# Two layers of mixed attention on one NeuronCore: another order of the paired attention steps

## The reference

```python
for layer in range(2):
    h = rmsnorm(x, norm_attn[layer]); proj = h @ w_in[layer]
    # four mixers of 4 heads each, head width 64
    o_sb = stick_breaking(q, k, v)   # a = exp(log_sigmoid(z) + suffix sums of -softplus(z)), strictly causal
    o_mb = softmax(q k^T * scale + bias, causal) @ v             # "moba": with 256 tokens its own block only
    o_ns = g0 * o_cmp + g1 * o_slc + g2 * o_win                  # one k/v head for each branch, sigmoid gates
    # cmp: keys and values from gelu(blocks @ w1) @ w2, 15 compressed positions
    o_df = rmsnorm((softmax1 - lam * softmax2) @ v) * (1 - lambda_init)
    x = x + concat(o_sb, o_mb, o_ns, o_df) @ w_out[layer]
    h2 = rmsnorm(x, norm_mlp[layer])
    x = x + relu(h2 @ w_up[layer])**2 @ w_down[layer]
x = rmsnorm(x, final_norm)
# second model: an mLSTM layer and a latent attention layer on x and 256 context tokens;
# each is steered by a modulation (silu(c) @ ada_w + ada_b), which does not depend on x
```

## Time and profile before

| | |
|---|---|
| median of three runs | 2309.01 us |
| time of the profiled execution | 2308.36 us |
| its span on the core | 2306.4 us |
| TensorE busy | 2208.7 us, 96% |
| VectorE busy | 1342.5 us, 58% |
| ScalarE busy | 1184.9 us, 51% |
| granted TensorE clock, mean | 0.99 of full |
| moved by DMA | 312.28 MB, 135 GB/s |

### The profile page before, as it was taken

How to read it: one execution, slowest core, us unless ns; L and a number is a source line. 1 busy time by engine, 2 the same in 40 slices (tenths; PEclk the granted TensorE clock), 3 DMA queues, 4 the chain that set the end, 5 groups by cost and what they waited for, 6 DMA issues and landing times.

```text
span 2306.4 us, 33632 instructions
## 1 busy us (share of the span) xinstructions
PE 2208.7 (96%) x13550; PEld 1833.3 (79%) x13550; DVE 1342.5 (58%) x2206; ACT 1184.9 (51%) x2004; POOL 0.2 (0%) x4
## 2 busy tenths in 40 slices
PE   8899999979999999999999999999999998899998
PEld 8669999849999777887677676868888876668998
DVE  5766645685654655445666654366666345546764
ACT  4665534575544654444344443266655336446764
POOL 0000000000000000000000000000000000000000
PEclk9899999989999999999999999999999999999999
DMA  8545575753576213222112121212223222214542
GB/s 307 203 182 182 215 307 197 280 204 131 182 291 241 91 55 114 87 100 98 58 73 73 73 74 46 101 70 95 92 93 108 92 73 92 92 38 150 184 169 101
DMA packets 45719, 312.28 MB, mean 135 GB/s; under 512 B 4951, under 2 KB 7255, under 8 KB 8580
## 3 DMA queue, kind: packets, MB, share of 16 engines
q1 hardware_dynamic: 45572, 310.20, 36.8%
HBM read 309.11 MB, written 1.07 MB: 134 GB/s over the span
## 4 chain that ended last, share of the span: by engine, by line
PE 82%; DVE 11%; ACT 5%; issue 2%; DMA 0%; ACTq 0%; DVEq 0%; SPq 0%
PE bank L792 62%; PE bank L797 8%; DVE ws L1775 2%; ACT ws L1301 2%; PE bank L1188 1%; PE bank L964 1%; DVE xs L1800 1%; PE bank L1159 1%; DVE hT L1931 1%; PE bank L865 1%; PE bank L1250 1%; PE bank L1120 1%; DVE arena L2203 1%; PE bank L1232 1%; PE bank L815 0%
## 5 line engine op out<-in xcount | busy, mean ns | idle before, releaser
L792 PE MATMUL bank<-xs,ws 128*128 128x256 f32 (+1 forms) x9648 | 1571.6, 324 | 34.3 <-DVE xs L1800 22.7
L792 PEld LDWEIGHTS bank<-xs,ws 128*128 128x128 f32 x9648 | 1399.0, 191 | 212.5 <-DVE xs L1800 36.9
L1775 DVE TENSOR_TENSOR ws<-ring,ws 128x1024 fp32r<-128x1024 f32 x464 | 547.8, 1222 | 303.8 <-ACT ws L1301 303.7
L1301 ACT ACTIVATE ws<-ring 128x1024 fp32r<-128x1024 f32 x464 | 464.7, 1050 | 304.0 <-PE bank L792 198.7
L1800 DVE TENSOR_TENSOR xs<-arena,xs 128x512 fp32r<-128x512 f32 (+1 forms) x286 | 162.3, 581 | 296.9 <-ACT xs L1325 295.4
L1325 ACT ACTIVATE xs<-arena 128x512 fp32r<-128x512 f32 (+1 forms) x286 | 149.0, 539 | 338.8 <-PE bank L792 226.9
L797 PE MATMUL bank<-ws,xs 128*128 128x512 f32 (+1 forms) x1008 | 230.1, 388 | 6.3 <-ACT arena L1580 2.2
L797 PEld LDWEIGHTS bank<-ws,xs 128*128 128x128 f32 x1008 | 188.4, 189 | 46.8 <-DVE xs L1800 3.2
L1325 ACT ACTIVATE xs<-hT 128x512 fp32r<-128x512 f32 (+1 forms) x216 | 122.8, 573 | 195.6 <-PE bank L792 186.7
L1800 DVE TENSOR_TENSOR xs<-hT,xs 128x512 fp32r<-128x512 f32 (+1 forms) x216 | 133.4, 620 | 153.4 <-ACT xs L1325 153.2
L1797 DVE SCALAR_TENSOR_TENSOR xs<-xT,par,xs 128x256 fp32r<-128x256 f32 x112 | 51.1, 479 | 11.8 <-ACT xs L1323 11.8
(11 more groups left out here) (259 smaller groups left out, 1355.9 us busy)
## 6 DMA issues: line engine op xcount, KB each, us to landing
ring<-in_stream SPq DMA_DIRECT2D x233, 1024.0 KB, 4.8
arena<-in_side SPq DMA_DIRECT2D x56, 1024.0 KB, 4.9
arena<-bias_vectors SPq DMA_DIRECT2D x1, 1536.0 KB, 9.1
hT<-in_tokens SPq DMA_DIRECT2D x1, 1024.0 KB, 6.1
arena<-in_tokens SPq DMA_DIRECT2D x1, 1024.0 KB, 13.6
out<-arena SPq DMA_DIRECT2D x2, 512.0 KB, 3.1
arena<-in_params SPq DMA_DIRECT2D x1, 918.0 KB, 9.4
arena<-bias_vectors SPq DMA_DIRECT2D x1, 706.0 KB, 10.5
```

The lines of the kernel that those rows point to most:

```text
L792: ins = mm(ps(n, c, c + g.T), a[wi][:, p * P:(p + 1) * P], x[xi], start=first, stop=last)
L1301: do(ws[:, i % 2, 0, c], ring[:, w % R, c], ACT.Copy).then_inc(w_high, 1)
L1775: ins = v.tensor_tensor(ws[:, i % 2, 1, c], ring[:, w % R, c], ws[:, i % 2, 0, c].bitcast(F32), ALU.subtract)
```

## The change

Seven things are done, all in the 14 attention steps of both layers. The moba pairs come first and the stick-breaking pairs after them (pairs 0, 1 and 2, 3). VectorE does the logits of the first unit of pair p, then finishes pair p-1, then does the logits of the second unit. The end of the gelu moves from p = 2 to p = 1, ahead of the finishing of pair 0. TensorE makes the compressed keys and values behind S at p = 3, not ahead. The `ada` units stand at the steps of `ADA_STEPS`: two at p = 2 (one ahead of the transposes), one at each of 3 to 10, none at 11 to 13, and one at 14 and 15. The call of `weights_to` for the second slot of `out` moves from p = 4 to the end of the loop. The buffers of the stick-breaking maps are indexed modulo 4, since their units have now the numbers 4 to 7.

```diff
-OUT_W_AT, OUT_X_AT = 4, 7
+OUT_X_AT = 7
-ADA_AT = 4
+ADA_STEPS = (2, 2, 3, 4, 5, 6, 7, 8, 9, 10, 14, 15)
@@ units(): the four "mb" units are appended first, then the four "sb" units
@@ ticket_plan(): the same moves
+            if p < NP:
+                n.add(("S", l, 2 * p), 1)
+                n.add(("S", l, 2 * p + 1), 1)
             if p == CMP_AT:
                 n.add(("kc", l))
                 n.add(("vc", l))
-            if p < NP:
-                n.add(("S", l, 2 * p), 1)
-                n.add(("S", l, 2 * p + 1), 1)
...
+            if p == ADA_STEPS[0]:
+                n.hold(("ada", l, 0))
             if p >= 2:
                 n.add(("PT", l, 2 * p - 4))
                 n.add(("PT", l, 2 * p - 3))
-            if p == ADA_AT:
-                n.hold(("ada", l, 0))
@@ TensorE: kc and vc go behind the products S, and
+                    if p == ADA_STEPS[0]:
+                        attention_ada(0)
                     if p >= 2:
                         for j in (2 * p - 4, 2 * p - 3):
...
-                    if ADA_AT <= p < ADA_AT + ADA_B:
-                        u = p - ADA_AT
...
+                    for u in range(ADA_B):
+                        if ADA_STEPS[u] == p and u > 0:
+                            attention_ada(u)
@@ ScalarE
-                    if p == OUT_W_AT:
-                        weights_to(G("out", l).s0 + 1)
                     if p == OUT_X_AT:
                         feed_to(G("out", l).q0 + 3, False)
...
                 squares(relu[:, 0, :].rearrange("p (a b) -> p a b", a=2), mixed[:, 6:8, :])
+                weights_to(G("out", l).s0 + 1)
@@ VectorE
                 for p in range(NP + 1):
-                    two = (2 * p, 2 * p + 1)
-                    for i in two if p < NP else ():
+                    for i in ((2 * p,) if p < NP else ()):
...                 (logits of that unit)
+                    if p == 1:
+                        dve.wait_ge(gelu_exp, l + 1)
...                 (the three operations that end the gelu, before at p == 2)
                     if p >= 1:
...                 (pair p-1 is finished)
+                    for i in ((2 * p + 1,) if p < NP else ()):
...                 (logits of that unit; then the parts of p == 0 and p == 1)
-                    if p == OUT_W_AT:
-                        weights_to(G("out", l).s0 + 1)
                     if p == OUT_X_AT:
...
+                weights_to(G("out", l).s0 + 1)
                 n = N(("O", l, NP - 1))
```

More of the change, by code:

```diff
@@ L115, in units @@
     for h in range(4):
+        out.append(dict(kind="mb", h=h, q=4 + h // 2, k=6 + h // 2, r=64 * (h % 2), kk=64, v=("vn", 1), bias=h,
+                        first=True, last=True, chunk=2 + h // 2, row=64 * (h % 2)))
+    for h in range(4):
         out.append(dict(kind="sb", h=h, q=h // 2, k=2 + h // 2, r=64 * (h % 2), kk=64, v=("vn", 0), first=True,
                         last=True, chunk=h // 2, row=64 * (h % 2)))
-    for h in range(4):
-        out.append(dict(kind="mb", h=h, q=4 + h // 2, k=6 + h // 2, r=64 * (h % 2), kk=64, v=("vn", 1), bias=h,
-                        first=True, last=True, chunk=2 + h // 2, row=64 * (h % 2)))
     for h0 in (0, 2):
@@ L976, in ada_turned, with attention_ada @@
                     ins.then_inc(bank_full[n % BANKS], 1)
-                for p in range(NP + 2):
[L979 to L992, removed]
+                def attention_ada(u):
+                    if l == u == 0:
+                        pe.wait_ge(cs_ready, seen(cs_ready))
+                    ins = ada_unit(("ada", l, 0), u, side_weights(l, CMP_W + u, KD))
+                    if u < ADA_B - 1:
+                        ins.then_inc(ada_done, 1)
+                    else:
+                        ins.then_inc(bank_full[N(("ada", l, 0)) % BANKS], N.turns(("ada", l, 0)))
+                for p in range(NP + 2):
                     if p < NP:
@@ L1012, in _ @@
                                     ins.then_inc(bank_full[n % BANKS], 1)
+                    if p == CMP_AT:
+                        pe.wait_ge(hid_ready, seen(hid_ready))
+                        n = N(("kc", l))
+                        pe.wait_ge(bank_free[n % BANKS], n // BANKS)
+                        for j in range(2):
+                            ins = mm(ps(n, 0, 16), par1_at(("w2k", l), 128 * j, 128), hidg[:, j, :],
+                                     start=(j == 0), stop=(j == 1))
+                        ins.then_inc(bank_full[n % BANKS], 1)
+                        n = N(("vc", l))
+                        pe.wait_ge(bank_free[n % BANKS], n // BANKS)
+                        for j in range(2):
+                            ins = mm(bank[n % BANKS][0:16, 0:64], hidg[:, 2 + j, :],
+                                     par1_at(("w2v", l), 64 * j, 64), start=(j == 0), stop=(j == 1))
+                        ins.then_inc(bank_full[n % BANKS], 1)
                     if l == 0 and p < 2:
@@ L1439, in _ @@
                                 act_.wait_ge(logits_ready, seen(logits_ready))
[L1440 removed]
+                                do(tbuf[:, i % 4, :], sbuf[:, i % 6, :], ACT.Abs).then_inc(act_own, 1)
                             for i in two:
                                 act_.wait_ge(act_own, own(act_own))
[L1443 removed]
+                                do(tbuf[:, i % 4, :], tbuf[:, i % 4, :], ACT.Exp, scale=-1.0).then_inc(act_own, 1)
                             for i in two:
                                 act_.wait_ge(act_own, own(act_own))
[L1446 removed]
+                                do(tbuf[:, i % 4, :], tbuf[:, i % 4, :], ACT.Ln, bias=one[:, :]).then_inc(exp_ready, 1)
                         for i in two:
```

123 lines of the change are left out of this document (66 added, 57 removed).

## The result

The changed kernel took 2322.92 us (median of six runs), the kernel before, run beside it, 2309.02 us (median of six, 2307.19 to 2316.70). Five of the six runs of the changed kernel lie from 2317.70 to 2323.12; the sixth, 2747.46 us at a mean clock of 0.748, is a slow run and is left out of the ratio. The ratio is 1.0046, with a 95% interval of 1.0030 to 1.0062: slower by 0.5%. Forecast were 2310.5 us and a range up to 2316.5, with 0.67 on no difference that can be measured.

What follows compares the result with a forecast made beforehand. TensorE bounds most of the kernel (96% busy); in the edited stage three engines are near each other, none full. Idle changes 0.0 and +0.7, plus 0.4 tail per layer, add 1.5 to 2308.4: 2309.9, median 2310.5, range 2302.5 to 2316.5.

Steps and rivals of the forecast that it cites:

- Front: Stage's start, p 0-3: VectorE idle 2.3 us ahead of unit 6 in layer 0, 1.4 in layer 1.
- Stick-breaking pairs: At p 3-5: VectorE waits of 1.2, 0.3 and 1.2 us (unit 10), 2.7 in each layer; bounds 1 and 4.
- first rival: Clock falls again in the middle, p 4-5: 2313 to 2316 us for one layer, 2316 to 2320 both; chance 0.18.
- Weights: Split of the second `out` slot moves from p 4 to p 7; waits there 0.75 and 0.6, 1.35 us in all.
- Finishing between the heads: Finishing pair p-1 between two units' logits: 0.7 us idle at p 7, 0.2 in the even part's ring.
- the ring of the even part: Logits, exponentials, PT copies, PV, S: 3.6 us, 3.9 with output copy, against VectorE's step of 3.4 to 3.5; 0.2 idle.
- the walk: Method for VectorE's idle times after the change: walking the three engine queues in program order, with durations from rows.
- Tail: From VectorE's finishing of pair 12 to the last PV: 5.5 us against 5.1 before, 0.4 more in each layer.
- Sum: Layer 0: 7.3 us idle against 7.3 before; layer 1: 6.4 against 5.7; 0.4 of tail in each; in all +1.5.

Runs made afterwards that it cites:

- warm_gaps: Changed kernel with 21 idle matmuls in each layer where TensorE waits: 2310.28 us, ratio 1.0002.
- no_p4_weights: Kernel before without the `weights_to` call at p = 4, so `feed_to` splits that slot at p = 7: 2313.82 us, ratio 1.0007.
- both_first: Changed kernel with VectorE's logits of both units ahead of the finishing, the other six edits kept: 2303.95 us, ratio 0.997.
- ada_even: Changed kernel with `ada` units at p = 11 to 13 and none at 7, 14 and 15: 2319.43 us, ratio 1.0041.
- the square: Order against idle matmuls: both_first 2303.95 and bf_warm 2299.49 us, changed kernel 2322.92 and warm_gaps 2310.28 us.
- the second set: Second of three sets of runs; the kernel before took 2311.95 us in it (27 runs).
- bf_ada_4_15: both_first with `ada` units at p = 4 to 15, as in the kernel before: 2313.04 us, ratio 1.0002.
- bf_ada_even: both_first with `ada` units at p = 11 to 13 and none at 7, 14 and 15: 2301.49 us, ratio 0.996.
- bf_warm: both_first with 15 idle matmuls in each layer: 2299.49 us, ratio 0.9945.
- bf_even_warm: both_first with the `ada` steps of bf_ada_even and 13 idle matmuls in each layer: 2299.42 us, ratio 0.9945.

## Why the prediction was wrong

By its own steps, layer 0 unless said:

- *Front.* 2.29 us idle ahead of unit 6 (2.3 forecast), nothing before it. Right, with the clock at the low level as assumed; in warm_gaps, where it is up, the wait is 0.93, which was the lower bound. In layer 1 it was 0.23 (1.4 forecast, bound 0).
- *Stick-breaking pairs.* 0.38 and 1.13 (0.3 and 1.2 forecast), and 2.43 ahead of unit 10 (1.2 forecast). The last is the first rival at its place: TensorE idle for 2.48 us until 110.88, the clock at 0.50 behind it. In layer 1 it came too, 2.75, and the term of 2.7 was 5.0 there. The 1.2 itself was right for full clock: in layer 1 of warm_gaps, with the clock at 1.00, the wait is 1.16 (the 1.97 of layer 0 stand behind idle matmuls at the low level). What the term lacked is the low clock at that place, 1.2 and 1.6 us.
- *Weights.* 0.95 and 0.42 (0.75 and 0.6 forecast), the split at p = 7 as foreseen. Right; and no_p4_weights shows that taking it away from p = 4 wins nothing by itself.
- *Finishing between the heads.* The wait at p = 7 is 0.73 (0.7 forecast). The step that failed is the ring of the even part, "0.2 idle in all by the walk; bounds 0 and 1.5": measured 4.16 and 4.60. At full clock it is 0.69, so that walk was short by half a microsecond; the other 3.5 to 4 are the clock. The walk had no slack in the ring at full clock and priced it there only; at the low level the ring is a microsecond or two longer, and nothing takes that up.
- *Tail.* From VectorE's last maximum (157.2) to the end of the last PV (164.6) it is 7.4 us (5.5 forecast), the first 4.5 of it at the low clock. In warm_gaps it is 5.7 (152.5 to 158.2).
- *Sum, layer 0.* 1.2 more up to p = 7, 4.0 in the even part, 1.9 in the tail: 7.1 of the 7.4 us by which the stage's growth (7.8) passed the forecast one (0.4). Against the waits that warm_gaps shows at full clock, 1.2, 3.5 and 1.7 of these, 6.4 in all, are the low clock. In layer 1 the idle time passed the forecast by 5.5 us: 2.3 more in the stick-breaking part and 4.4 in the even part, 1.2 less in front.

The first rival, that the clock falls again, had the right mechanism, 0.18, and 2313 to 2320, still 3 us below what was measured. It was tied to one place, p = 4, and priced once in each layer. The rule of the Trainium skill that the prediction quoted (TensorE: Matmul & The Clock Gate, "HAM oscillation — how this bites in real kernels") has idle gaps between groups of products that put the array back to the low clock. In the case that the Trainium skill tells there, the gaps are waits of some 3 to 5 us for DMA. This trace agrees in kind, and at shorter gaps, 1.61 us (until 150.94) and 2.48 us (until 110.88), with 0.51 and 0.50 behind them. That every gap is paid twice, as the prediction put it, is more than the Trainium skill says of gaps this short, and the trace doesn't show it: 0.92 us of idle time (until 130.73) had 1.00 behind it. Of two gaps of 2.51 us before, one had a fall behind it; the changed kernel has gaps at many steps, and I counted one.

Where the clock is held up, the changed kernel takes 2310.28 us, which is the forecast's 2310.5; but there the front of layer 0 is at full clock too, where the forecast took the low one, and the idle matmuls add waits of their own, so the agreement is partly luck. What the sum didn't ask is what the same walk gives in the other order: in layer 0 both_first has none of the waits of 2.29 (unit 6), 0.38, 1.13 and 0.73. The "no change" of the forecast was a gain of some 7 us by six edits (0.3%) against a loss by one that is larger alone, and only their difference was in view.

What stays open: why the clock falls at some gaps and not at others of the same length (0.98 us until 121.75, with a fall at 124; 0.92 until 130.73, with none), and why whole runs of one kernel differ in it (below). How much of the 3.5 us of ada_even is real was not tried with more runs, and the square was not run with the same idle matmuls in both orders.

## What to carry to other kernels

Where several engines pass work around in a ring, compute the ring at the low clock as well: if it has no slack there, an idle gap of TensorE can be paid again by the ring that follows. An engine that produces for others should hand out both inputs before it turns to its own finishing: in both kernels where it was tried, the other order cost 12.7 and 19.0 us. And put independent TensorE work, useful work first, where TensorE waits: 15 idle matmuls in a layer gave back 4.5 us and the early start of the modulation 7 to 9.

## What the runs showed of the hardware

- The spread between runs of one kernel goes with the clock; what moves the clock from run to run is not known. The runs of the second set show it most plainly: bf_ada_4_15 took 2306.6 us at a mean clock of 0.988 and 2316.0 at 0.983; bf_ada_even 2298.7 to 2299.5 at 0.994 and 2303.5 to 2306.1 at 0.990 to 0.992. Whether a kernel with filled gaps scatters less is not shown: bf_warm lies within 2.9 us and bf_ada_4_15 within 9.4, but bf_even_warm, filled too, within 7.3 and ada_even, not filled, within 2.5.
- Added matmuls that compute nothing made a kernel faster: 21 in each layer, 84 records that keep TensorE busy for 25.1 us in all, won 12.6 us by the medians (10 by the ratios), since most of them lay in idle time.
- The clock also fell behind gaps shorter than 2.51 us. In the changed kernel TensorE stood at 0.98 from 144.70 to 151.70, idle for 2.34 us of these 7.00 in all, with its last gap, 1.61, ending at 150.94, and at 0.51 from 151.70 to 161.70, where it worked almost without pause (9.33 of 10.00 us). Before, gaps of 2.51 us were followed by either level.
